# One hybrid decoder step: sample-state products turned around, g and beta spread from rows, the output matrix fetched last

## The reference, cut to what matters

```
h = rms(x);  p = h @ w_in                       # q,k,v of two branches, gates, alpha, beta
branch A (gated delta rule, 4 heads, 128x128 state per head and sequence)
    w, u from a triangular solve;  v_new = u - w @ S
    o = (q e^g) @ S + attn @ v_new;  S = S e^glast + kd^T @ v_new
branch B (GLA, 4 heads, 64x128 state)
    o = attn @ v + (q e^g) @ S;      S = S e^glast + kd^T @ v
merged = sigmoid(gate_a) * (o_a @ w_up_a) + sigmoid(gate_b) * (o_b @ w_up_b)
x = x + merged @ w_o
x = x + MoE(rms(x))                             # 32 experts, top 4, 1024 -> 2x1024 -> 1024
```

## Time and profile before

| | |
|---|---|
| runs shown | 1423.0, 1426.0, 1426.69 us |
| profiled execution | 1425.51 us, span 1423.8 us |
| TensorE matmul busy | 1332.6 us (94%) |
| VectorE / ScalarE / GpSimd busy | 427.4 / 295.4 / 30.2 us |
| moved by DMA | 447.71 MB, mean 314 GB/s |
| weights of the experts | 192 fetches of 2 MB |

### The profile page before, as it was taken

How to read it: one execution, slowest core, us unless ns; L and a number is a source line. 1 busy time by engine, 2 the same in 40 slices (tenths; PEclk the granted TensorE clock), 3 DMA queues, 4 the chain that set the end, 5 groups by cost and what they waited for, 6 DMA issues and landing times.

```text
span 1423.8 us, 15834 instructions
## 1 busy us (share of the span) xinstructions
PE 1332.6 (94%) x5945; PEld 643.0 (45%) x5945; DVE 427.4 (30%) x796; ACT 295.4 (21%) x528; POOL 30.2 (2%) x67
## 2 busy tenths in 40 slices
PE   6999989989899999999999999999999999999996
PEld 5777779854555433333333333333333333333332
DVE  3436346048012332132123221232212312132123
ACT  2474441230002211111102111021110211111202
POOL 4000000000100000000000000000000000000000
PEclk9999979978999899999999999999999999999999
DMA  9522200122733699999999999999999999999993
GB/s 278 158 87 65 89 30 1 60 66 77 270 152 136 261 417 428 429 429 428 429 428 429 429 428 429 428 429 428 429 429 428 428 429 429 428 429 428 429 429 145
DMA packets 61833, 447.71 MB, mean 314 GB/s; under 512 B 7597, under 2 KB 30201, under 8 KB 37228
## 3 DMA queue, kind: packets, MB, share of 16 engines
q1 hardware_dynamic: 59820, 440.34, 75.1%
q0 software_dynamic: 1984, 6.98, 1.4%
HBM read 442.29 MB, written 5.02 MB: 314 GB/s over the span
## 4 chain that ended last, share of the span: by engine, by line
PE 47%; DMA 46%; DVE 4%; ACT 1%; issue 1%; SPq 0%; DVEq 0%; ACTq 0%
DMA ring<-in_w_gate_up_dram 45%; PE bank L614 17%; PE bank L566 14%; PE bank L920 2%; PE bank L1000 2%; DMA ring<-in_w_up_b_dram 1%; PE bank L789 1%; PE bank L628 1%; PE bank L801 1%; PE bank L721 1%; PE bank L873 1%; PE bank L797 1%; PE bank L741 1%; PE bank L900 1%; PE bank L951 0%
## 5 line engine op out<-in xcount | busy, mean ns | idle before, releaser
L614 PE MATMUL bank<-ring,zgb 128*64 128x512 f32 x2560 | 565.7, 596 | 45.9 <-DMA ring<-in_w_gate_up_dram 37.0
L614 PEld LDWEIGHTS bank<-ring,zgb 128*64 128x64 f32 x2560 | 179.5, 137 | 428.8 <-issue 329.5
L1812 DVE COPY zgb<-bank 128x512 f32<-128x512 f32 x32 | 22.1, 692 | 636.9 <-PE bank L614 636.9
L566 PE MATMUL bank<-hTb,ring 128*128 128x320 f32 x640 | 181.5, 443 | 1.4 <-DVE hTb L1452 1.4
L566 PEld LDWEIGHTS bank<-hTb,ring 128*128 128x128 f32 x640 | 123.6, 195 | 52.9 <-issue 3.9
L614 PE MATMUL bank<-ring,cv 128*64 128x512 f32 x512 | 116.9, 598 | 0.0
L1380 ACT COPY zgb<-bank 128x512 f32<-128x512 f32 x32 | 18.7, 586 | 419.4 <-PE bank L614 419.4
L1000 PE MATMUL bank<-h2b,Sl 128*128 128x512 f32 (+1 forms) x204 | 85.6, 628 | 0.0
L1390 ACT COPY hTb<-bank 64x512 f32<-64x512 f32 x64 | 37.1, 579 | 197.4 <-PE bank L614 196.4
L1029 PE MATMUL bank<-hTb 128*128 128x512 f32 x136 | 68.2, 606 | 0.0
L1787 DVE TENSOR_TENSOR xbuf<-xbuf,bank 128x512 f32<-128x512 f32 x85 | 58.4, 688 | 20.0 <-PE bank L614 11.2
(11 more groups left out here) (377 smaller groups left out, 1033.6 us busy)
## 6 DMA issues: line engine op xcount, KB each, us to landing
ring<-in_w_gate_up_dram SPq DMA_DIRECT2D x128, 2048.0 KB, 23.6
ring<-in_w_down_dram SPq DMA_DIRECT2D x64, 2048.0 KB, 20.6
ring<-in_w_in_dram SPq DMA_DIRECT2D x22, 1024.0 KB, 5.5
ring<-in_w_o_dram SPq DMA_DIRECT2D x4, 1024.0 KB, 10.0
ring<-in_w_up_a_dram SPq DMA_DIRECT2D x2, 1024.0 KB, 5.0
ring<-in_w_up_b_dram SPq DMA_DIRECT2D x2, 1024.0 KB, 12.1
out_dram<-Sg POOLq DMA_DIRECT2D x1, 2048.0 KB, 16.9
xbuf<-in_x_prompt_dram SPq DMA_DIRECT2D x2, 512.0 KB, 4.0
```

The costliest lines, as they stand in the source:

```text
L566: mm = pe.matmul(o[0:m, 0:TOK], w[:, k, c0:c0 + m], rhs[:, k, :], start=(k == 0), stop=(k == kk - 1))
L614: mm = pe.matmul(o[64 * f:64 * f + 64, 0:width], lhs, w[f] if isinstance(w, list) else w[:, width * f:width * f + width], start=start, sto ...
L1812: link(V.tensor_copy(pre[:, 1, :], bank[PRE[1]][:, :]), pre_done[1], n * 2 + (x + 1))
```

## The change

- Start: the x rows are scaled and turned first. `cols` is turned between the first and the second tile of x and waits only for the five row loads; the convolution state has a semaphore of its own and is turned after `qkv0`.
- g and beta: six matmuls with `g_tm`/`beta` as stationary operand (4 columns) make rows in two banks (`gbr`, `bbr`); ScalarE copies them into `gb_rows` (4 partitions each); per head one matmul with a selector of 4 rows (`sel`, made by GpSimd) spreads the row over 128 partitions.
- Branch B's sample rows: the rows are the stationary operand (32 columns: four sequences) and the four sequences' states move (512 columns). Four such blocks stand in a bank's four quarters of partitions. VectorE keeps each row's own sequence (`pick`: a multiplication by a mask, then a sum over four), and one matmul with the identity adds it to the output (`Xl`). The products stand after `g0` and `gla_out(0)`.
- Branch A's sample rows: the same, `k20` to `k23`, 16 matmuls ahead of `gb0`, picked by VectorE into `Xg`. `rt2` follows `rt1`, `v2` follows `v1`, `o2` follows `s1`, and the gates stand between them.
- New sample states: `spread` makes [64, 4x128] matrices (two of each kind, used in turn); each `ss`/`gss` matmul contracts over 32 rows.
- `w_o` is fetched after the last panel. The prompt state is written after `s1`.

```diff
 def psum_order():
-    o = ["cols", "cst"]
-    o += [f"xT{s}{f}" for s in range(3) for f in range(2)]
-    o += [f"qkv{t}" for t in range(QT)]
+    o = ["xT00", "xT01", "cols", "xT10", "xT11", "xT20", "xT21", "qkv0", "cst"]
+    o += [f"qkv{t}" for t in range(1, QT)]
...
+        VM = [[flat(ring, W0 + 3072 + 1024 * i + 512 * k, (4, 128)) for k in range(2)] for i in range(2)]
+        picked = [flat(ring, W1 + 512 * k, (4, 128)) for k in range(2)]
...
@@ SyncE
-                if i == P_M + 8:
-
-                    sp.wait_ge(o_ready, 2)
-                    full(sp, f"gss{HEADS - 1}1")
-                    for k in range(WO):
-                        src = w_o[0][256 * k:256 * k + 256, :].rearrange("(k p) n -> p k n", p=128)
-                        sp.dma_start(slot(MIX + k).rearrange("p (k n) -> p k n", k=2), src).then_inc(wfull[MIX + k], 16)
+            sp.wait_ge(o_ready, 2)
+            full(sp, f"gss{HEADS - 1}1")
+            for k in range(WO):
+                src = w_o[0][256 * k:256 * k + 256, :].rearrange("(k p) n -> p k n", p=128)
+                sp.dma_start(slot(MIX + k).rearrange("p (k n) -> p k n", k=2), src).then_inc(wfull[MIX + k], 16)
@@ TensorE
                         if s == 2:
-                            for b in range(BATCHES):
-                                mm = pe.matmul(o[:, hp, 8 * b:8 * b + 8], Sl[64 * r:64 * r + 64, 2 * b + hp, :],
-                                               eq[64 * r:64 * r + 64, hp, a + 8 * b:a + 8 * b + 8], start=False,
-                                               stop=True, skip_group_check=True)
+                            pe.wait_ge(xl_ready, r + 1)
+                            mm = pe.matmul(o[:, hp, 0:n], Xl[:, r, :], ident[:, 64 * hp:64 * hp + 64], start=False,
+                                           stop=True)
...
+            o = take("gbr")
+            for s in range(3):
+                n, a = TILE_N[s], TILE_0[s]
+                mm = pe.matmul(o[0:HEADS, a:a + n], g_tm[0:n, s, :], (triu if s < 2 else tri8)[0:n, 0:n], start=True,
+                               stop=True)
+            done(mm, "gbr")
...
+            def gla_states():
+
+                a = PROMPT
+                o = [take("oi0"), take("oi1")]
+                Sl4 = Sl[:, :, :].rearrange("p (b a) e -> p b a e", a=2)
+                for hp in range(2):
+                    for th in range(2):
+                        c = 32 * (2 * hp + th)
+                        for r in range(2):
+                            u = slice(64 * r, 64 * r + 64)
+                            mm = pe.matmul(o[r][c:c + 32, :], eq[u, hp, a + 32 * th:a + 32 * th + 32],
+                                           Sl4[u, 4 * th:4 * th + 4, hp, :], start=True, stop=True)
...
             for h in range(HEADS):
-                for nm, col in (("gB", g_tm), ("bB", beta)):
+                for nm, r in (("gB", 0), ("bB", 32)):
                     o = take(f"{nm}{h}")
-                    for s in range(3):
-                        n = TILE_N[s]
-                        rhs = ident if nm == "bB" else (triu if s < 2 else tri8)
-                        mm = pe.matmul(o[:, TILE_0[s]:TILE_0[s] + n], col[0:n, s, h:h + 1].to_broadcast([n, 128]),
-                                       rhs[0:n, 0:n], start=True, stop=True)
-                    done(mm, f"{nm}{h}")
+                    done(pe.matmul(o[:, 0:TOK], sel[r:r + HEADS, h, :], gb_rows[r:r + HEADS], start=True, stop=True),
+                         f"{nm}{h}")
...
             new_values(0)
+            Sg4 = Sg[:, :, :].rearrange("p (b h) e -> p b h e", h=HEADS)
+            for h in range(HEADS):
+                o = take(f"k2{h}")
+                for z in range(2):
+                    for th in range(2):
+                        c = 32 * (2 * z + th)
+                        mm = pe.matmul(o[c:c + 32, :], kbqg[:, z, h, PROMPT + 32 * th:PROMPT + 32 * th + 32],
+                                       Sg4[:, 4 * th:4 * th + 4, h, :], start=True, stop=True)
+                done(mm, f"k2{h}")
             gate("gb", 0)
...
             rhs_rows(1, LT[:, 1, :, :], 0)
+            rhs_rows(2, qkv[:, 8:12, :], PROMPT)
             gate("ga", 2)
             new_values(1)
+            new_values(2)
             gate("gb", 2)
             gdn_out(1)
             new_state(1)
-            o = take("ks2")[:, :].rearrange("p (h z t) -> p h z t", h=HEADS, z=2)
-            for h in range(HEADS):
-                for b in range(BATCHES):
-                    mm = pe.matmul(o[:, h, :, 8 * b:8 * b + 8], Sg[:, HEADS * b + h, :],
-                                   kbqg[:, :, h, PROMPT + 8 * b:PROMPT + 8 * b + 8], start=True, stop=True)
-            done(mm, "ks2")
-            freed(pe, "ks2")
-            rhs_rows(2, LT[:, 2, :, :], 0)
-            new_values(2)
             gdn_out(2)
...
-                        done(pe.matmul(o[:, :], kdT[0:64, 2, m, :], VM[0][0:64, 4 * f:4 * f + 4, :], start=True,
-                                       stop=True), f"ss{m}{f}")
+                        u = slice(32 * f, 32 * f + 32)
+                        done(pe.matmul(o[:, :], kdT[u, 2, m, :], VM[0][m % 2][u, :, :], start=True, stop=True), f"ss{m}{f}")
@@ VectorE
+            def pick(name, k, dst, signal):
+
+                o = p3(full(dve, name), 4, 128)
+                free(TTo(picked[k][:, :, :], o, last(m4[:, :], 128), ALU.mult), name)
+                step(V.reduce_sum(dst, picked[k][:, :, :].rearrange("p b e -> p e b"), AX_X), signal)
...
+            for h in range(HEADS):
+                pick(f"k2{h}", h % 2, Xg[:, h, :], xg2_ready)
...
-                    step(TTo(VM[i][0:64, :, :], mid(v, BATCHES), last(bsel[0:64, :], 128), ALU.mult), vm_ready)
+                    step(TTo(VM[i][h % 2][0:64, :, :], mid(v, 4), last(m4[0:64, :], 128), ALU.mult), vm_ready)
```

More of the change, by code:

```diff
@@ L73, in psum_order @@
         o += [f"L{lv}{s}{r}" for s in range(3 if lv == 0 else 2) for r in range(2)] + fill[lv]
-    o += [f"gT{s}" for s in range(3)]
+    o += [f"gT{s}" for s in range(3)] + ["gbr", "bbr"]
     for h in range(HEADS):
@@ L89, in psum_order @@
                 o += ([f"Y{s}{b}"] if b != levels_of(s)[-1] else []) + [f"Z{s}{b}"]
-    o += ["rt0", "ga0", "v0", "gb0", "o0", "s0", "ga1", "ks1", "gb1", "rt1", "ga2", "v1", "gb2", "o1", "s1", "ks2",
-          "rt2", "v2", "o2", "ga3"] + [f"on{h}" for h in range(HEADS)] + ["gb3"]
+    o += ["rt0", "ga0", "v0"] + [f"k2{h}" for h in range(HEADS)]
+    o += ["gb0", "o0", "s0", "ga1", "ks1", "gb1", "rt1", "rt2", "ga2", "v1", "v2", "gb2", "o1", "s1", "o2", "ga3"] + [f"on{h}" for h in range(HEADS)] + ["gb3"]
     for m in range(KD):
@@ L570, in _ @@
             pe.wait_ge(consts, 2)
[L571 to L577, removed]
             for s in range(3):
+                if s == 1:
+                    pe.wait_ge(s_rows, 16 * 5)
+                    o = take("cols")
+                    done(pe.transpose(o[:, 0:60], rows[0:60, :], ident[0:60, 0:60]), "cols")
                 n = TILE_N[s]
@@ L591, in _ @@
                 done(fm(f"qkv{t}", t // 2, 128 * (t % 2), hT), f"qkv{t}")
+                if t == 0:
+                    pe.wait_ge(s_cst, 16)
+                    o = take("cst")
+                    for j in range(QT):
+                        mm = pe.transpose(o[:, 24 * j:24 * j + 24], cst_rows[:, 128 * j:128 * j + 128], ident[0:24, 0:24])
+                    done(mm, "cst")
             pe.wait_ge(s_small, 48)
@@ L1436, in _, with rows_scaled @@
             step(V.memset(kdf[:, :, :], 0.0))
-            o = full(dve, "cols")
-            free(V.tensor_copy(cols[:, 0:60], o[:, 0:60]), "cols")
-            step(V.memset(cat[:, :, 0:3], 0.0))
-            o = full(dve, "cst")
-            v = cat[:, :, CATS:CATN].rearrange("p t (b w) -> p t b w", w=3 + STEPS)[:, :, :, 0:3]
-            free(V.tensor_copy(v, o[:, 0:24 * QT].rearrange("p (t b w) -> p t b w", t=QT, w=3)), "cst")
-            for s in range(3):
+            def rows_scaled(s):
                 n = TILE_N[s]
@@ L1447, in _, with turned @@
                 step(TS(x_tm[0:n, s, :], x_tm[0:n, s, :], rs[0:n, s:s + 1], None, ALU.mult), xs_ready)
-            for s in range(3):
+            def turned(s):
                 n, a = TILE_N[s], TILE_0[s]
@@ L1453, in _ @@
                          f"xT{s}{f}")
+            rows_scaled(0)
+            step(V.memset(cat[:, :, 0:3], 0.0))
+            rows_scaled(1)
+            o = full(dve, "cols")
+            free(V.tensor_copy(cols[:, 0:60], o[:, 0:60]), "cols")
+            turned(0)
+            rows_scaled(2)
+            turned(1)
+            turned(2)
+            o = full(dve, "cst")
+            v = cat[:, :, CATS:CATN].rearrange("p t (b w) -> p t b w", w=3 + STEPS)[:, :, :, 0:3]
+            free(V.tensor_copy(v, o[:, 0:24 * QT].rearrange("p (t b w) -> p t b w", t=QT, w=3)), "cst")
             for t in range(QT):
@@ L1583, in _ @@
                 step(TTo(kbqg[:, 0, h, :], kbqg[:, 0, h, :], oA[:, h, :], ALU.mult), kb_ready)
```

(4 more changed lines are left out.)

102 lines of the change are left out of this document (65 added, 37 removed).

## The result

Four executions of the changed kernel took 1381.4 to 1385.51 us, median 1382.39, against 1424.98 (1423.0 to 1426.69) for the kernel before: ratio 0.9706, 95% interval 0.9694 to 0.9718. The profiled execution is the longest of the four, 1385.51 us with a span of 1383.4.

The account below looks back on a forecast made before the run. TensorE's chain bounds the mixer up to expert 0, DMA the loop from 660 us on. Gains 2.4 + 11.6 + 10.5 + 0.5 + 9.1 = 34.1 us give 1391.4, median 1391.9 us; range 1379 to 1410.

Parts of the forecast that it names:

- Where the time hangs: From expert 0 to the end: 945.2 us stay, so each microsecond the mixer gives up comes off the whole.
- Start: Start of the kernel: `qkv0` starts at 13.6 instead of 17.48 us; gain 2.4 us, bounds 0 to 3.9.
- g, beta and branch B: g, beta and branch B's sample rows: 48.2 us fall to 36.6 at full clock; gain 11.6 us.
- Branch A: Branch A's sample rows, to the end of `ga3`: 25.3 us fall to 14.8; gain 10.5 us.
- Sample states: New sample states: TensorE starts `ss1` 0.5 us earlier, half clock stays; gain 0.5 us.
- 32 instead of 64 rows contracted: same moving columns, same price: New sample states: matmuls over 32 rows cost the same as over 64, so no gain from them.
- I leave the half clock in: New sample states: the half-clock stretch after an idle gap stays; gain 0.5 us, without it 4.3.
- Order of fetches: `w_up_b` queued ahead of `w_o`: the 6.4 us stall and 2.7 us of clock loss go; gain 9.1 us.
- Rival 1: Better cover: fours side by side (-5.2) and full clock in the sample-state rounds (-3.8): 1382.9 us; chance 0.20.
- Rival 2: Sample rows of branches B and A: the clock falls all the same; 1410.7 us, or about 1401 for one; chance 0.14.
- Rival 3: Reordered fetch: GpSimd's 2 MB store holds `w_up_b` up as `w_o` did; 9.1 us back, 1401.0; chance 0.07.
- rival 4: Turned-around sample products: records run one at a time and at half clock; slower than before, about 1432 us; chance 0.03.

Follow-up runs that it names:

- e1: Changed kernel with the old order at the start, both row loads' turns ahead of x: 1383.68 us, ratio to the kernel before 0.9708.
- e2: Changed kernel with unread identity matmuls filling TensorE's gaps ahead of `qkv0`: 1379.35 us, ratio to the kernel before 0.9679.
- e7: Changed kernel with branch B's sample product as before, 64x128 states stationary and 8 moving columns: 1392.11 us, ratio to the kernel before 0.9771.
- e9: Changed kernel with shape-test groups of 8 matmuls ahead of `k20`: (a) same 32 columns, (b) four column groups in turn, (c) same 32 rows; total 1444.99 us.
- e4: Changed kernel with branch A's 16 products reordered, four heads in a row on the same 32 columns: 1389.06 us, ratio to the kernel before 0.9756.
- e8: Changed kernel with new sample states contracted over 64 rows as before, spread over 8 blocks: 1390.21 us, ratio to the kernel before 0.9760.
- e10: Changed kernel with branch A's 16 products replaced by 32 matmuls, 128x128 states stationary, 16 moving columns: 1392.81 us, ratio to the kernel before 0.9765.
- e5: Changed kernel with the old order of fetches, `w_o` ahead of the second up matrix: 1394.58 us, ratio to the kernel before 0.9786.
- e6: Kernel before with the new order of fetches alone, `w_o` last: 1417.07 us, ratio to the kernel before 0.9947.
- e3: Changed kernel with 9, 3 and 1 unread matmuls ahead of the waits for `t2t_ready`: 1382.02 us, ratio to the kernel before 0.9709.

## Why the prediction was right, and where it was off

**Where the time hangs.** Right: 945.2 us from expert 0 to the end in both kernels.

**Start.** The step failed in sign: forecast a gain of 2.4 us, measured -0.5 in the profile, and none by e1. `qkv0` started at 14.14, close to the forecast 13.6. What failed is the price of what comes then: the 16 records were taken at 4.3 us, as at full level, and took 7.3, the first ten of them at half (e2). The forecast had no term for the level here. The column for the clock doesn't show it either: the changed kernel's profile carries 1.00 over the first 22 us, although durations up to about 19.5 us are those of the half level.

**g, beta and branch B.** The mechanism was right, the forecast 4.4 us short. Mis-sized terms: the product at 1.1 us instead of 3.5, and the four spreads at 0.8 instead of 1.1, since the selector's 4 rows for g and for beta start at rows 0 and 32 and so run side by side as well: their records start in pairs, under 0.01 us apart. The full clock, on which 8.7 us of the forecast rested, came as forecast (1.00), and e7 shows why.

**Branch A.** Right in kind, 2.1 us short: the product at 3.6 instead of 7.0 (e9, b), against `o2`, which took 2.9 instead of 1.9. Its 16 records come in turn from products over 64 rows and over 128, and two of them take 0.36 us; in `o1`, where all go over 128 rows and move twice the columns, two take 0.22. The forecast had taken the price of the latter kind; why the alternation costs more isn't tested. The strided sum, which no row had shown, took 1.03 to 1.09 us (0.7 by the nearest row, and nothing in the sum); the cover held.

**Inverse of branch A.** Forecast untouched, 3.2 us longer in the profiled execution, from a clock of 0.91 instead of 0.97 (0.09 x 56.1 - 0.03 x 52.9 = 3.5 us). By e1, e2, e4 and e7 its size varies from run to run.

**Sample states.** The step that was furthest off: 6.2 against 0.5. Two of its terms failed. One is "32 instead of 64 rows contracted: same moving columns, same price". A pair on rows 0 to 31 and 32 to 63 runs side by side: 1.13 against 1.98, four rounds, two kinds, some 7 us on TensorE. The other is "I leave the half clock in". From one `ss` to the next, and from the last to the end of `ga4`, the kernel before took 11.1, 13.3, 8.3 and 8.2 us, the changed one 10.6, 8.8, 8.8 and 6.5. So 4.5 of the 6.2 us come from the second round, which lay at half level for some 10 us before and ran at 1.00 now. 1.7 come from the last, where the pairs count in full, and 0.5 from the first. The third is 0.5 longer, because VectorE's round of 8.8 us, forecast as 8.7, is now the pace. The half level hasn't gone from the stretch (0.92 over all of it, 0.89 before): it now falls on rounds in which TensorE has time to spare. e8 brings the long stretch at half level back, but doesn't show which part of its change does it.

**Order of fetches.** Right: 9.4 against 9.1; `w_o` was not late, and no wait of TensorE for it appears.

**Rivals.** Rival 1 named both things that happened: four and more side by side, and a full clock in the sample-state round that had been at half. That its sum (1382.9) met the median (1382.4) so closely is partly chance. It lacks the shorter spreads and the pairs in the sample states, and against them the 2.9 us that the start fell short and the 3.2 of the inverse; and the profile, by which these are counted, is 3.1 us above the median. Rival 2 didn't occur in either product; e7 and e10 show what it would have been in the old form. Rival 3 is excluded by e5 and e6, and rival 4's condition, records one at a time, by e9.

## What to carry to other kernels

Where a matmul uses few rows or columns of the array, spread neighbours in the list over distinct row and column groups: the count of groups nearly divides the time (7.05, 3.70, 1.92, 1.09 us in e9), and the order in the list alone was worth more than twofold (e4). Column groups shared a bank here; row groups had a bank each, and one bank for both wasn't tried. Where few rows meet many matrices, let the matrices move and keep the rows stationary; it was less work here, and it also avoided the long streams of weight loads in which the clock fell (e7, e10). On a queue in order, ask of each large fetch who needs it first.

## What the runs showed of the hardware that wasn't expected

- Row groups run side by side as column groups do: 16 records of 512 columns take 7.05 us on one group, 3.70 on two, 1.92 on four, 1.09 on eight (e9).
- The level fell without any idle gap: in streams of full loads with 8 or 16 moving columns (e7, e10) and in a stream that held only 32 rows of the array (e9, c: clock 0.76), while a stream of the same length on one group of 32 columns stayed at full level (e9, a). Those of e9 are single stretches of one execution.
- Banks in turn don't help on the same columns: records 0.43 us apart in e4, as in e9, a.
- Small products over 64 and 128 rows in turn cost more than those over 128 alone: 0.36 us for two records against 0.22 (`o2` and `o1` in the changed kernel).
- Matmuls that nobody reads paid: 3 to 4 us at the start (e2). Elsewhere the gain is smaller than what one profile suggests (e3), since the half-level stretches vary from execution to execution.
